# The recurrent heads' latent projections in three pairs of seven half products, their weight sums on GpSimd, and the raw stream loaded again and turned during the merge

## The reference

```python
p = h @ w_in                      # 1024 x 12800, split into 14 parts
# parts 0..4: q, z forward, z backward, value i, readout gate g (8 heads of 128)
# parts 5..7: the convolution branch
k = (1 - lb) * sigmoid(-z);  f = lb + (1 - lb) * sigmoid(z)
ol_f, _ = hgrn_direction(ql, zl_f, il, lb_fwd, sc_f, False)   # gated linear recurrence
ol_b, _ = hgrn_direction(ql, zl_b, il, lb_bwd, sc_b, True)
a = rmsnorm(ol_f + ol_b) * silu(g)
b = p5 * depthwise_conv3(p6 * p7)
c = attention(...)                                            # 16 heads, 4 key heads
y = sigmoid(ga) * (a @ w_a) + sigmoid(gb) * (b @ w_b) + sigmoid(gc) * (c @ w_c)
x = x + gain * (y @ w_out)
```

## Time and profile before

| | us |
|---|---|
| three runs, median (lowest, highest) | 2879.82 (2878.57, 2880.78) |
| the profiled execution | 2880.71 |
| its span, first to last instruction | 2878.9 |
| PE busy in it | 2760.4 (96%) |
| DVE / ACT / POOL busy | 1109.8 / 511.8 / 0.2 |

### The profile page before, as it was taken

How to read it: one execution, slowest core, us unless ns; L and a number is a source line. 1 busy time by engine, 2 the same in 40 slices (tenths; PEclk the granted TensorE clock), 3 DMA queues, 4 the chain that set the end, 5 groups by cost and what they waited for, 6 DMA issues and landing times.

```text
span 2878.9 us, 29819 instructions
## 1 busy us (share of the span) xinstructions
PE 2760.4 (96%) x11866; PEld 1648.3 (57%) x11866; DVE 1109.8 (39%) x2108; ACT 511.8 (18%) x883; POOL 0.2 (0%) x4
## 2 busy tenths in 40 slices
PE   7999999999899999999699999989989999999997
PEld 3566665666644444444334433334387786888886
DVE  3143444444434344311411111145274235654654
ACT  2121111111233233211100000022222103100001
POOL 0000000000000000000000000000000000000000
PEclk9999999999999999999899999999999999999999
DMA  9611111101111121132699999952101431333330
GB/s 324 230 50 54 51 55 51 55 26 37 30 56 47 45 59 45 51 102 61 235 409 409 409 409 409 409 174 60 44 1 47 129 103 30 88 88 88 88 86 33
DMA packets 327140, 372.41 MB, mean 129 GB/s; under 512 B 10017, under 2 KB 273014, under 8 KB 323702
## 3 DMA queue, kind: packets, MB, share of 16 engines
q1 hardware_dynamic: 326758, 369.83, 37.4%
q10 hardware_dynamic: 272, 1.05, 0.1%
HBM read 368.75 MB, written 2.10 MB: 129 GB/s over the span
## 4 chain that ended last, share of the span: by engine, by line
PE 93%; DVE 3%; DVEq 1%; DMA 1%; ACT 1%; issue 1%; SPq 0%; ACTq 0%
PE psum L1430 17%; PE psum L681 15%; PE psum L1738 12%; PE psum L1264 8%; PE psum L1894 6%; PE psum L1365 4%; PE psum L672 3%; PE psum L1004 2%; PE psum L1623 2%; PE psum L1399 2%; PE psum L754 2%; PE psum L2425 2%; PE psum L1664 2%; PE psum L1194 2%; PE psum L1243 1%; PE psum L1223 1%
## 5 line engine op out<-in xcount | busy, mean ns | idle before, releaser
L1430 PE MATMUL psum<-arena 128*128 128x256 f32 x2240 | 484.5, 378 | 0.5 <-ACT arena L2523 0.5
L1430 PEld LDWEIGHTS psum<-arena 128*128 128x128 f32 x2240 | 422.8, 189 | 61.9 <-ACT arena L2523 0.7
L681 PE MATMUL psum<-arena 128*128 128x512 f32 (+1 forms) x1152 | 455.3, 546 | 1.5 <-DVE arena L607 1.5
L1738 PE MATMUL psum<-arena 128*64 128x512 f32 x1536 | 347.6, 597 | 3.0 <-issue 2.1
L681 PEld LDWEIGHTS psum<-arena 128*128 128x128 f32 x1152 | 213.3, 190 | 202.8 <-issue 192.1
L1264 PE MATMUL psum<-arena 128*128 128x512 f32 x512 | 233.1, 597 | 0.0
L1738 PEld LDWEIGHTS psum<-arena 128*64 128x64 f32 x1536 | 104.8, 136 | 217.6 <-issue 214.5
L1894 PE MATMUL psum<-arena 128*128 128x512 f32 (+1 forms) x448 | 168.9, 535 | 0.0
L1264 PEld LDWEIGHTS psum<-arena 128*128 128x128 f32 x512 | 92.4, 189 | 104.1 <-issue 104.1
L1669 DVE SCALAR_TENSOR_TENSOR arena<-psum,arena 128x512 f32<-128x512 f32 x64 | 48.1, 751 | 246.4 <-PE psum L1664 245.8
L1894 PEld LDWEIGHTS psum<-arena 128*128 128x128 f32 x448 | 85.3, 191 | 83.0 <-issue 79.6
(11 more groups left out here) (358 smaller groups left out, 2965.9 us busy)
## 6 DMA issues: line engine op xcount, KB each, us to landing
arena<-in_w_gate SPq DMA_DIRECT2D x64, 1024.0 KB, 18.3
arena<-in_w_up SPq DMA_DIRECT2D x64, 1024.0 KB, 16.3
arena<-in_w_down SPq DMA_DIRECT2D x64, 1024.0 KB, 18.0
arena<-in_w_in SPq DMA_DIRECT2D x120, 512.0 KB, 3.8
arena<-in_ada_w SPq DMA_DIRECT2D x24, 1024.0 KB, 7.5
arena<-in_w_up SPq DMA_DIRECT2D x32, 512.0 KB, 5.2
arena<-in_w_down SPq DMA_DIRECT2D x32, 512.0 KB, 4.4
arena<-in_w_out SPq DMA_DIRECT2D x16, 512.0 KB, 3.8
```

The costliest lines, as they stand in the source:

```text
L681: mm = pe.matmul(bank[:, 0:b - a], w[:, k, :], HT[:, k, a:b], start=(k == 0), stop=(k == KC - 1))
L1430: mm = pe.matmul(psum[:, base + b, c * HALF:(c + 1) * HALF], w, v, start=(first and q == 0 and m in (0, 2, 3, 4)), stop=(last and q == KC ...
L1738: mm = pe.matmul(psum[64 * e:64 * e + 64, bank + n, :], tokens(e, 2 * q + k), w[:, k, 512 * n:512 * n + 512], start=(q == 0 and k == 0), s ...
```

## The change

It has five parts.

1. For each head, the pairs (b6, b7), (b5, g) and (zf, zb) of latent projections go through `pe_seven` with banks 0 to 3 (`pe_hg_quad`). In head 0 the first pair stays plain. ACT copies a quarter of the result, and DVE recombines it into `hq_o` in SBUF; the convolution, the silu and the sigmoids read from there. The two context gates are one bank of two plain halves (`pe_hg_gates`); values and query stay plain.
2. Weight sums of these pairs are made on GpSimd (`pool_hg`): four adds or subtracts of 128 x 512 for a pair. The fourth sum overwrites half of the second weight, so for the pair (zf, zb) it waits for `head_gates`.
3. Token sums of `HT` are made once, at the end of `dve_first`, and lie in the place of `XT`.
4. Levels stand at other places of the loop: level 0 ahead of the first pair, most others inside a pair, by the quarter `q` of `pe_seven`.
5. `XT` isn't filled in setup. After the last use of `aT` in attention, SP loads `x` again (2 MB), and during the merge PE turns it by four transposes behind each of eight pieces, and DVE copies.

```diff
-        def pe_turn_tile(pe, n):
...
-            for n in range(LT):
-                pe_turn_tile(pe, n)
             pe.wait_ge(sem("rows1_in"), 16 * N_ROWS1)
...
+            dve.drain()
+            for q in range(KC // 2):
+                token_sums(dve, HT[:, 2 * q:2 * q + 2, C:T], ht_t[:, q])
+            dve.sem_inc(once("ht_sums"), 1)
...
+        def hg_sums(g):
+            kept = hq_sums[g % 2]
+            even = hg_pair(g)[1].rearrange("p (k h) n -> p h k n", h=2)[:, 0]
+            return [kept[:, 0], kept[:, 1], kept[:, 2], even]
+
+        def pool_hg_sums(pool, i, g):
+
+            for e in range(2):
+                ws.arrived(pool, "hg", i, 2 * g + e)
+            if g == 0:
+                done(pool, "hg", i - 1, 5)
+            if g == 1 and not is_first(i):
+                done(pool, "hg", i - 1, 3)
+            if g == 2:
+                if not is_first(i):
+                    done(pool, "hg", i, 1)
+                pool.wait_ge(sem("head_gates"), i + 1)
+            weight_sums(pool, *hg_pair(g), hg_sums(g), "hq_sums")
...
+        def pe_hg_quad(pe, i, g, within):
+
+            for e in range(2):
+                ws.arrived(pe, "hg", i, 2 * g + e)
+            pe.wait_ge(sem("hq_sums"), i * 3 + g)
+            pe.wait_ge(sem("hq_out"), i * 3 + g)
+            if g == 0:
+                pe.wait_ge(sem("head_query"), i)
+            pe_seven(pe, *hg_pair(g), hg_sums(g), HT[:, :, C:T], ht_t, 0, True, True, within)\
+                .then_inc(sem("weights_used"), 2)
...
+                pe_level(pe, i, 0)
+                pe_hg_quad(pe, i, 0, levels({3: 1}))
+                pe_hg_gates(pe, i, lambda: pe_level(pe, i, 2))
+                pe_hg_quad(pe, i, 1, levels({1: 3, 3: 4}))
+                pe_level(pe, i, 5)
+                pe_hg_values(pe, i, 0)
+                pe_hg_quad(pe, i, 2, levels({1: 6, 3: 7}))
+                pe.wait_ge(sem("head_values_out"), i * 2 + 1)
+                pe_turn_keys(pe, i)
+                pe_hg_values(pe, i, 1)
+                pe_states(pe, i)
...
+                pe_hg_query(pe, i, outputs)
+                pe_head_norm(pe, i)
...
+                dve_level(dve, i, 1)
+                dve_hg_quad(dve, i, 0)
+                dve_level(dve, i, 2)
                 dve_conv1(dve, i)
-                dve_level(dve, i, 1)
+                dve_level(dve, i, 3)
+                dve_level(dve, i, 4)
+                dve_hg_quad(dve, i, 1)
+                dve_level(dve, i, 5)
                 dve_conv2(dve, i)
-                for l in range(2, 8):
-                    dve_level(dve, i, l)
+                dve_level(dve, i, 6)
+                dve_level(dve, i, 7)
+                dve_hg_quad(dve, i, 2)
                 dve_states(dve, i)
...
+        def sp_x_again(sp):
+            done(sp, "attn", 0, unit_of_fill(4 * KC - 3))
+            sp.dma_start(x_again, A["x"][0].rearrange("(t p) d -> p t d", p=P)).then_inc(sem("ctx_in"), 16)
+
+        def pe_turn_stream(pe, k):
+
+            if k == 0:
+                pe.wait_ge(sem("ctx_in"), 32)
+            wait(pe, sem("turn_out"), NT + k - 1)
+            for t in range(LT):
+                mm = pe.transpose(psum[:, 2 + k % 2, t * P:(t + 1) * P], x_again[:, t, k * P:(k + 1) * P], ident)
+            mm.then_inc(sem("turned"), 1)
...
+                if 2 <= n < 2 + KC:
+                    pe_turn_stream(pe, n - 2)
...
+        def weight_sums(eng, wa, wb, sums, formed):
 
             a, b = (w.rearrange("p (k h) n -> p h k n", h=2) for w in (wa, wb))
-            dve.tensor_tensor(sums[:, 0], b[:, 0], b[:, 1], ALU.add)
...
+            eng.tensor_tensor(sums[0], b[:, 0], b[:, 1], ALU.add)
+            eng.tensor_tensor(sums[2], a[:, 0], b[:, 0], ALU.subtract)
+            eng.drain()
+            eng.tensor_tensor(sums[1], sums[0], a[:, 0], ALU.subtract)
+            eng.drain()
+            eng.tensor_tensor(sums[3], a[:, 1], sums[1], ALU.subtract)
+            eng.drain()
+            eng.sem_inc(sem(formed), 1)
...
+        def recombine(dve, base, a, u, o):
...
-        POOL_STEPS = []
+        POOL_STEPS = [pool_hg]
```

More of the change, by code:

```diff
@@ L637, in mixed_block_kernel @@
         hw_s = hgp.take(10, P)
[L638 to L640 removed]
+        hw_r = aT[:, KC - 1, :]
+        hw_sq = hw_r
+        hw_o = hw_r
+        hq_u = hgp.take(HALF + S)
+        hq_o = hgp.take(2 * S)
+        hq_sums = [hgp.take(3 * 4, P).rearrange("p (m k) n -> p m k n", m=3) for _ in range(2)]
+        HG_END = CT_LO + 19444
         FWD_TILES = [0, 1, 2, 3, 4]
@@ new lines, in pool_hg, with pe_hg_plain @@
+        def pool_hg(pool):
+            for g in (1, 2):
+                pool_hg_sums(pool, 0, g)
+            with pool.Fori(1, HEADS) as i:
+                for g in range(3):
+                    pool_hg_sums(pool, i, g)
+        def pe_hg_plain(pe, u):
+            ws.arrived(pe, "hg", 0, u)
+            for k in range(KC):
+                pe.wait_ge(sem("first_normed"), k + 1)
+                mm = pe.matmul(psum[:, u, :], ws.dst("hg", u)[:, k, :], HT[:, k, C:T], start=(k == 0), stop=(k == KC - 1))
+            mm.then_inc(sem("weights_used"), 1)
@@ new lines, in pe_hg_gates @@
+        def pe_hg_gates(pe, i, between):
+            if not is_first(i):
+                pe.wait_ge(sem("head_out"), i)
+            for d in range(2):
+                ws.arrived(pe, "hg", i, 4 + d)
+                for k in range(KC):
+                    if is_first(i) and d == 0:
+                        pe.wait_ge(sem("first_normed"), KC + k + 1)
+                    mm = pe.matmul(psum[:, gates_bank(i), d * C:(d + 1) * C], ws.dst("hg", 4 + d)[:, k, :], HT[:, k, 0:C],
+                                   start=(k == 0), stop=(k == KC - 1))
+                if d == 0:
+                    between()
+            mm.then_inc(sem("head_gates"), 1)
@@ new lines, in pe_hg_query, with act_hg_copy @@
+        def pe_hg_query(pe, i, within=None):
+            ws.arrived(pe, "hg", i, 7)
+            pe.wait_ge(sem("hq_out"), i * 3 + 3)
+            for k in range(KC):
+                mm = pe.matmul(psum[:, 0, :], ws.dst("hg", 7)[:, k, :], HT[:, k, C:T], start=(k == 0), stop=(k == KC - 1))
+                if within is not None and k == KC - 3:
+                    within()
+            mm.then_inc(sem("weights_used"), 1)
+        def act_hg_copy(act, i, g):
+            done(act, "hg", i, 2 * g + 1)
+            if g:
+                act.wait_ge(sem("hq_read"), i * 2 + g)
+            if is_first(i) and g == 0:
+                act.activation(hq_o[:, 0:S], psum[:, 0, :], ACT.Copy)
+                act.activation(hq_o[:, S:2 * S], psum[:, 1, :], ACT.Copy).then_inc(sem("hq_copied"), 1)
+            else:
+                act.activation(hq_o[:, 0:HALF], psum[:, 0, 0:HALF], ACT.Copy).then_inc(sem("hq_copied"), 1)
```

305 lines of the change are left out of this document (149 added, 156 removed).

## The result

The changed kernel took 2854.59 us, the median of 4 runs (2853.33 to 2855.79), beside 2879.2 for the kernel before on the same chip: a ratio of 0.9915, interval 0.9897 to 0.9932. In a second group of runs, five of each kernel or more, it was 2853.92 beside 2877.74, ratio 0.9921, interval 0.9908 to 0.9935. So it is 24 us faster. Forecast were 2861 and a range of 2852 to 2876: the sign and the range hold, and the number is 6.4 too high, at rival B's 2855.5.

What follows compares the result with a forecast made beforehand. PE was taken as the bound, busy 96% of the span. From 2880.7 us, -34.2 - 3.3 + 6.9 + 2.8 + 5.3 + 3.5 = -19.0 gave 2861.7, forecast as 2861, range 2852 to 2876.

Steps and rivals of the forecast that it cites:

- rival B: GpSimd's sums don't disturb DVE at all in the rounds: -24.3, 2855.5 us; chance 0.25.
- I take p = 1.0: p, us a GpSimd sum keeps DVE out; four delay level 3 by 4p: 0.75 per round, 5.3 in all.
- The prediction's other estimate, 1.35: p by the Trainium skill's lockout and 1.96 times DVE's time: 1.35 us, costing 15 us instead of 5.3.
- The margin of 3.25: Walk through one round's timing from the first quad's end: level 3 on DVE may be 3.25 us late.
- Level 5's wait: In each round level 5 is due only a quarter after level 4: PE waits 0.4 us, 2.8 in all.
- Level 0's wait: At the round's start level 0 waits for dve_begin, only pe_head_norm between: 0.8 us, six rounds, 4.8.
- Level 0 in round 1: dve_begin is held back by modulation vectors that DVE finishes first: PE waits 2.1 us.
- The merge: 32 transposes added on PE cost 3.5 us in full; DVE's copies and the load are free.
- Head 0's late `ada_w`: 16 late uses keep their pace except at the gates, where 1 us may be lost; only in the range.
- C: Rival: full lockout by GpSimd operations twice as long as DVE's, p = 1.4: 16.5 instead of 5.3, 2872; chance 0.20.
- D: Rival: a further 1 to 2 us of waits per round in the level chain: 2875, up to 2882; chance 0.09.
- E: Rival: slower, sums hold DVE long and level 4 waits for level 3; p = 2.5 gives 2903; chance 0.06.

Runs made afterwards that it cites:

- e1: Changed kernel without the GpSimd weight sums in rounds 1 to 7 (only signalled, stale sums used): 2851.63 us, ratio 0.9907.
- e2: Changed kernel with each of GpSimd's weight sums done twice in a row: 2899.05 us, ratio 1.007.
- e4: Changed kernel with level 0 behind the first quarter of the first pair and level 1 behind that pair: 2862.85 us, ratio 0.9943.
- e6: Changed kernel without the merge's 32 transposes and eight DVE copies (residual added to stale data): 2852.27 us, ratio 0.9908.
- e8: e4 with GpSimd's sums of the last pair held until DVE has finished level 4: 2850.55 us, ratio 0.9908; again 2851.3, ratio 0.9905.
- e3: Changed kernel with the weight sums made by DVE instead of GpSimd, a little ahead of need: 2855.59 us, ratio 0.9921.

## Why the prediction was right, and where its number was off

- **PE is the bound and a removed matmul is gained**: right. A quarter takes 3.02, a round 77.02. 34.2 us were to come in the rounds, and 26.0 of them remain after the waits; forecast was 21.3 (26.6 without interference), the 2.1 of round 1's level 0 not counted, since it lies ahead of the round.
- **The step that was mis-sized is "I take p = 1.0"**, worth 5.3 us. It measured 0.67, and since 4p has to pass 3.25 before it costs anything, the term is 0, not two thirds of 5.3. The row I had the earlier trace rows gave 0.69, and I moved away from it for an overhead that no row showed. But that row was right by luck: it is DVE's own time for a sum, and what a DVE operation loses is the rest of the GpSimd operation it meets, 0.55 to 1.08 in these runs. The prediction's other estimate, 1.35, is a whole operation of GpSimd; the four arrived midway. The margin of 3.25, worked out by the walk, was nearly right (3.1 by e1): e2 (twice the sums) and e4 (less margin) both passed it and waited.
- **The whole miss.** The profiled execution is 6.3 under the sum's 2861.7. Terms of the sum give -5.3 here, -1.7 (level 5), +0.7 and +0.3 (level 0 in six rounds and in the tail) and +2.9 (level 0 in round 1), each as below: -3.1 together. The rest is outside the sum: +3.1 (`ada_w`), -2.0 (the slow first piece before), -1.6 (setup), -1.2 (attention) and -1.7 (`w_out`), -3.4 together, and none of it is shown to be the change's. So half of the miss is the sum's, and that the mis-sized term alone has nearly the size of the miss is chance.
- **Level 5's wait**, 0.4 per round: 0.13 to 0.16. 1.7 less over seven rounds.
- **Level 0's wait**, 0.8 per round: 0.92 in six rounds, 0.7 more.
- **Level 0 in round 1**, 2.1: 3.6, and a second price. The sums for round 1 fall on `dve_begin`, which I had looked at only as a reader of the modulation vectors. DVE's operations there are longer (the first is 0.17 without a sum beside it, the second 0.43), PE waits, and then the clock is 0.72, with 0.50 from 125 to 127:

```profile
121.64 1.01 DVE L504 SCALAR_TENSOR_TENSOR arena<-arena 128x8 f32<-128x8 f32 x1
...
122.88 1.26 DVE L821 COPY arena<-arena 128x512 f32<-128x512 f32 x1
```

```profile
124.83 2.08 PE L811 MATMUL psum<-arena 128*128 128x128 f32 x8 [3.59 <-DVEq L823]
```

```profile
125.00:126.00 1.00, 1.00 (x5) 1.00 (x6) 0.96 (x2) 0.00 (x0) 0.00 (x0) 0.50 0.00 0
124.00:130.00 6.00, 5.17 (x22) 4.70 (x23) 5.42 (x10) 0.00 (x0) 0.00 (x0) 0.72 0.00 0
130.00:136.00 6.00, 6.00 (x29) 5.27 (x28) 0.35 (x2) 0.00 (x0) 0.00 (x0) 1.00 0.01 3
```

  2.08 for 1.16 and 9.51 for 9.07 are 1.4 us of clock on top of the wait. e1, without most of the sums, waits 1.91 and has neither. With these the rounds close: -34.2 + 6 x 0.92 + 7 x 0.15 + 1.4 and 0.3 for the tail's level 0 (0.92 for 0.62) make -25.9, measured -26.0. In all, this place cost 3.6 + 1.4 = 5.0 where 2.1 stood in the sum. 1.7 + 1.4 = 3.1 of it are the sums' by e1, whose median is 3.0 lower.
- **The merge**: +3.5 forecast, +3.5 measured, and e6 gives it back. No wait for weights.
- **Head 0's late `ada_w`**, "I leave it out of the sum": 0.2 and 3.1 us in the two profiles of the changed kernel, both with a fast first piece; what decides isn't shown.
- **Rival B** (no disturbance) gave the number, for a reason that is wrong: there is disturbance. **C** asked for p = 1.4, twice what came on average; the lockout that it named is there. **D** held only in e4's order of the work. **E**'s place and mechanism appeared in e2, but no wait came from it in the changed kernel.

What stays open: whether any of the 1.0 to 1.6 us in the setup is the change's, what makes the first piece slow in some profiles, and what sets the waits for `ada_w`.

## What to carry to other kernels

Price work put on a second engine by the slack of what it runs beside, not by its own length: the same four GpSimd operations cost 0 or 1.8 us per round, depending on whether DVE had 3 us to spare there. What a DVE operation loses is the rest of the GpSimd operation it meets. Look for every place at which the new work comes to lie, the first, irregular round above all, which here cost 3.1 us, where the 28 regular operations of the last pairs cost none. And before explaining a difference of 2 us between two profiles, take a second profile of each.

## What the runs showed of the hardware

- A sum of two 128x512 tensors takes GpSimd 1.09 to 1.28 us where DVE takes 0.69, a ratio of 1.6 to 1.9; a pair's four, start to start of the next, take 188.57 - 183.27 = 5.3, against DVE's 2.84 with drains. The Trainium skill ("GPSIMD Engine Reference", Elementwise — side-by-side cycle accounting) gives 1.96 at 2048 elements; these, at 512, are somewhat under it.
- DVE operations from SBUF to SBUF that meet a sum on GpSimd are lengthened whatever their size: a 128x8 one from 0.17 to 1.01, a copy of 128x512 from 0.43 to 1.26, others by 0.55 to 1.1. In the eight rows of the changed kernel's round 2 and of e4 they end 0.13 to 0.21 before the end of the GpSimd operation they met, plus their own undisturbed length. Two copies of 128x8 at 122.57 and 122.65, between two sums, keep their 0.16. One with an operand in PSUM beside a sum is not lengthened (0.73 at 241.74 in e8, 0.72 without).
- Behind a wait of PE at level 0 of 2.2 us or more the granted clock was lower for some microseconds (0.72 over 6 us, with 0.50, which is 1.2 GHz, in the middle), worth 1.4 to 1.7 us. Ahead of these waits PE had run four transposes (round 1) or the query's and outputs' products (e2). Behind level 4's wait of 2.73 in e2, ahead of which it had run half products, the clock stayed at 1.00, and behind waits of 0.92 too. With 1.91 it came once (e3, where level 0 took 2.08) and once not (e1, 1.16). Behind the wait of 1.96 at `w_out`, ahead of which PE had run products of 512 columns, the 1.7 us came in eight of 14 profiles. So the length of the wait alone doesn't decide, nor, by these rows, the kind of work ahead of it.
